# A two-block transformer step on one core: gate products in rounded parts, other banks and another order in the sparse attention, and one high part moved in the memory attention

## The chip, the cores and the metric

The kernel is one program on 1 core of a Trainium2 chip. The metric is the device time of one execution, in microseconds (us). The engines are PE (TensorE), DVE (VectorE), ACT (ScalarE), POOL (GpSimd) and SP (SyncE, which issues most of the weight loads).

## The reference, cut to what matters

`reference` runs two blocks on x of 512 tokens by 1024 features, all in float32. The first is a feed-forward layer, a mixer (retention and differential attention), memory attention and a second feed-forward layer. The second block begins with one wide product, whose parts feed sparse attention (compressed, selected and window branches), a gated recurrence ("mlstm"), a second memory attention and a merge; a feed-forward layer ends it. The change touches these lines:

```python
# memory attention of the first block: per head, a query product, its norm, softmax, values
q = rms_norm((h @ w_q).reshape(b, s, MEM_HEADS, MEM_HEAD_DIM), q_norm)
p = jax.nn.softmax(sc, axis=-1).astype(v.dtype)
# second block: gates, and the recurrence's running maximum
gb = jax.nn.sigmoid(g_nsa.reshape(B, S, NSA_GROUPS, NSA_HPG, 3))
gates = if_ml.astype(jnp.float32) + ml_gate_b[l].astype(jnp.float32)
logf = jax.nn.log_sigmoid(gates[..., ML_HEADS:])
b = jnp.cumsum(fj, axis=1).transpose(0, 2, 1)
m_t = jnp.maximum(inter, jnp.max(dlog, axis=-1))
# compressed scores of a group of four heads; with 512 tokens every block is selected
s = jnp.einsum('bsghd,bngd->bghsn', q, kc) * NSA_SCALE
y_nsa = (gb[..., 0:1] * o_cmp + gb[..., 1:2] * o_slc + gb[..., 2:3] * o_win).reshape(B, S, NSA_Q)
```

## The kernel before, in words

All activations lie transposed in SBUF. A weight panel (128 output columns, 8 tiles of 128 rows) is loaded by SP into a ring of `slot`s and split into a rounded high part and a rounded low part (`parts0` and `parts1` in turn). The high part is made by ACT (`high_part`, L2020) or by POOL (L574), the low part always by POOL (L586, or L583 and L586 in two pieces). A panel product on PE is then 24 matmuls in rounded float32: high and low against the activations' high part `hhi`, high against their low part `hlo`. Matmuls on plain float32 operands are one instruction in the code and two records in the trace.

The order on every engine is written out by hand, and semaphores count banks, panels and steps. `emptied(b, n)` lets PE wait until bank b was read n times in this stage; `Counts` and dictionaries such as `NSA` hold how often each is counted per stage.

Gates stage (`n.past(KV2)` to `n.past(GATES)`): PE makes four group products, and between them the gate product (`gate_w` against `h32`, plain float32), a cumulative sum (`lf` against `tables`, twice, and `ifp` against the identity), and columns of the result (`gate_columns`). DVE makes the running maximum in `rows`. Ahead of the stage DVE scales x by the norm (L3208).

Sparse stage: 4 groups of 4 heads. A group needs three panels (two of queries, one of keys), whose product goes to bank c % 2. ACT copies out the rounded high part (`query_or_key`), then DVE the low part (`query_low`, L3260) and frees the bank; the keys are then copied to the other 64 partitions by two DMAs of ACT's queue (`key_twins`). The selected and window branches run in 64 steps s, 16 per group. In a step PE makes `sparse_scores(s)`, DVE its minima (`sparse_minima`, L3328), ACT the exponentials (L2586), and DVE the probabilities (`sparse_probs(s - 1)`, L3340). PE turns those of step s - 2 (`turn_sparse`, L1675), ACT places them (`place_sparse`, L2013), and every fourth step has a `sparse_out` (L1690, L1693). Between them PE weaves matmuls of the next panels, whose number per step stands in `V_FILL` (group 0), `FILL` (groups 1 and 2) and a fixed 3 (group 3). The compressed branch of a group is `compressed_scores` (L1644), then DVE's front, maxima, ACT's exponential, DVE's back and division, then `turn_compressed`. The steps p = 13 to 15 of a group have no woven matmuls.

Recurrence: `spread_maxima` (L1767) brings a row of the running maximum to all partitions, once per head.

Of the kernel before, what the change touches and what calls it, by code (L numbers as in the profile page):

```python
# [27 lines left out]
P = 128  # L28
# [77 lines left out]
NSA = dict(products=16, splits=16, highs=16, free0=8, free1=10, free2=9, qkhighs=3 * GROUPS, free3=STEPS, free4=STEPS,  # L106
           free5=STEPS, free6=STEPS, free7=1 + 2 * GROUPS, twins=GROUPS, cscores=GROUPS, cmps=GROUPS, cexps=GROUPS,
           cprobs=GROUPS, cturned=GROUPS, scores=2 * STEPS, exps=2 * STEPS, probs=2 * STEPS, turned=2 * STEPS, outs=8,
           dve=7 * GROUPS + STEPS)
FILL = [(6, 0)] + [(3, 3)] * 6 + [(3, 2)] * 6  # L110
# [3 lines left out]
FREED = (0, 0, 1, 3, 3, 4, 4, 6, 5, 7, 7, 8)  # L114
CBANK, CFREED = (1, 1, 0, 1), (1, 5, 6, 9)
# [24 lines left out]
GATES = dict(outs=1, free7=1, gates=1, acts=5, free2=1, dve=4, stats=2, free3=2, turned=1, free6=1)  # L140
# [65 lines left out]
def build(nc, xT, memT, mem2T, par, con, tab, headtab, w8, w7, w4, gatew, cmpw1, cmpw2, outT):  # L206
    with ExitStack() as ctx:
# [36 lines left out]
        gate_w = sb("gate_w", KD, GATE_COLS)  # L244
# [15 lines left out]
        lf = sb("lf", 4, TT, 4)  # L260
# [26 lines left out]
        rows = hid[:, 18:22, :]  # L287
        PTr = hid[:, 8:12, :]
# [57 lines left out]
        cmp_loaded = sem("cmp_loaded")  # L346
        shifted = sem("shifted_rows_copied")
# [63 lines left out]
        zeros_set = sem("zeros_set")  # L411

# [130 lines left out]
        def _(pool):  # L543
# [107 lines left out]
            for p in range(30):  # L651
                split(p, p % RING, "act" if 10 <= p < 28 else p - 2 if p < 2 else p - 1, load=1 + p // RING, pieces=2 if p >= 8 else 1)
# [37 lines left out]
            pool.memset(ssum[:, :], 0.0).then_inc(zeros_set, 1)  # L690
            n.past(KV2)
# [35 lines left out]
        def _(pe):  # L727
# [779 lines left out]
            def gate_columns():  # L1507

                emptied(6, 1)
                emptied(3, 1)  # L1510
                for t in range(TT):
# [7 lines left out]
            pe.wait_ge(cmp_loaded, 96)  # L1519
# [17 lines left out]
            for t in range(TT):  # L1537
                mm = pe.matmul(bank[3][0:4, t * P:T], lf[:, 1, t, :], tables[:, K_CUM:K_CUM + T - t * P],
                               start=(t == 0), stop=(t == TT - 1))
            mm.then_inc(stats, 1)  # L1540
            emptied(6)
            for t in range(TT):
                pe.matmul(bank[6][0:4, t * P:T], lf[:, 2, t, :], tables[:, K_CUM:K_CUM + T - t * P],
                          start=(t == 0), stop=False)
# [63 lines left out]
            def sparse_values(q, a, b):  # L1608
# [4 lines left out]
                for m in range(a, b):  # L1613
                    t, j = (m // 4, m // 2 % 2) if m < 16 else ((m - 16) // 2, m % 2)
                    at = (0, 1, 2, 7)[t]
                    if q == 0 and m < 16 and m % 4 == 0:
                        emptied(at, (2, 2, 0, 1)[t])
# [2036 lines left out]
```

## Time and profile before

| | |
|---|---|
| median of 3 runs | 2387.17 us (2385.77 to 2392.31) |
| profiled execution, its time | 2383.35 us |
| its span | 2381.5 us |
| PE busy | 2304.9 us (97%) |
| DVE, ACT, POOL busy | 898.9, 884.1, 1029.8 us |
| gates stage (PE) | 1235.17 to 1273.16 us |
| sparse stage (PE) | 1273.16 to 1555.4 us |

The span is the profiler's stretch from first to last instruction, and the execution's own time is 1.85 us more. Times in rows are counted from the span's start. A row of the timeline has its start, its length, the engine, the line and the operation; the brackets give the idle time before it and what ended that. PEclk is the granted TensorE clock, where 1.00 is 2.4 GHz and 0.50 is 1.2 GHz.

### The profile page before, as it was taken

The page shows a single profiled execution, that of the slowest core. Times are in us where ns is not written, and L with a number is a line of the kernel's source. Part 1 is how long each engine was busy: PE and PEld are TensorE (multiplying, and loading weights), DVE is VectorE, ACT ScalarE, POOL GpSimd, SP SyncE. Part 2 cuts the span into 40 slices and gives each one's busy share as a digit, 9 for nine tenths or more (in the row PEclk, how much of TensorE's full clock was granted, in tenths as well). Part 3 has the DMA queues.
Part 4 walks back from the last instruction along what each step waited for, and adds up shares of the span by engine and source line. Part 5 has one row for each costly group of instructions (what it writes and reads, how often), then busy time and mean ns, then how long its engine had stood idle before and what let it go on. Part 6 is the DMA issues. An engine that isn't in the chain of part 4 may idle for free.

```text
span 2381.5 us, 28274 instructions
## 1 busy us (share of the span) xinstructions
PE 2304.9 (97%) x10592; PEld 1843.2 (77%) x10592; DVE 898.9 (38%) x1499; ACT 884.1 (37%) x1566; POOL 1029.8 (43%) x560
## 2 busy tenths in 40 slices
PE   7999999999999999999999999999999998999997
PEld 6888888777687788888867766677788877888886
DVE  4443424024422344533233566635511113333411
ACT  4222334245544532223323465645522234222332
POOL 3444457832362544444534422053244443444445
PEclk9999999999999999999999999999999998999998
DMA  4333334322231233323352211021123331333232
GB/s 170 96 96 96 95 94 151 118 73 66 68 98 45 73 96 97 97 88 93 102 142 83 63 38 35 18 71 62 45 89 98 96 97 54 97 97 97 83 95 96
DMA packets 81259, 206.39 MB, mean 87 GB/s; under 512 B 7440, under 2 KB 31120, under 8 KB 80912
## 3 DMA queue, kind: packets, MB, share of 16 engines
q1 hardware_dynamic: 72832, 191.92, 26.3%
q10 hardware_dynamic: 8336, 13.25, 1.9%
q8 instruction: 58, 0.95, 0.2%
q14 instruction: 33, 0.27, 0.0%
HBM read 199.71 MB, written 2.10 MB: 85 GB/s over the span
## 4 chain that ended last, share of the span: by engine, by line
PE 89%; ACT 4%; DVE 4%; POOL 1%; issue 1%; ACTq 0%; DMA 0%; DVEq 0%; POOLq 0%
PE bank L769 16%; PE bank L770 15%; PE bank L776 15%; PE bank L1071 5%; PE bank L1937 3%; PE bank L1938 3%; PE bank L1942 3%; PE bank L1304 3%; PE bank L1563 2%; PE bank L1742 2%; PE bank L1693 2%; PE bank L1664 1%; PE bank L1619 1%; PE bank L1675 1%; PE bank L1756 1%; PE bank L1848 1%
## 5 line engine op out<-in xcount | busy, mean ns | idle before, releaser
L586 POOL TENSOR_TENSOR parts<-slot,parts 128x1024 fp32r<-128x1024 f32 (+3 forms) x318 | 634.8, 1996 | 629.7 <-ACT parts L2020 628.0
L769 PE MATMUL bank<-hhi,parts 128*128 128x512 f32 x1440 | 562.3, 390 | 6.2 <-POOL parts L586 3.5
L2020 ACT ACTIVATE parts<-slot 128x1024 fp32r<-128x1024 f32 (+2 forms) x281 | 271.9, 968 | 781.7 <-PE bank L776 734.4
L770 PE MATMUL bank<-hhi,parts 128*128 128x512 f32 x1440 | 561.3, 390 | 0.0
L776 PE MATMUL bank<-hlo,parts 128*128 128x512 f32 x1440 | 356.7, 389 | 0.0
L769 PEld LDWEIGHTS bank<-hhi,parts 128*128 128x128 f32 x1440 | 270.8, 188 | 67.3 <-issue 7.0
L770 PEld LDWEIGHTS bank<-hhi,parts 128*128 128x128 f32 x1440 | 270.9, 188 | 55.7
L776 PEld LDWEIGHTS bank<-hlo,parts 128*128 128x128 f32 x1440 | 270.2, 188 | 56.1
L574 POOL TENSOR_TENSOR parts<-slot,lanes 128x1024 fp32r<-128x1024 f32 x42 | 83.5, 1988 | 285.9 <-PE bank L1563 127.0
L2866 DVE TENSOR_TENSOR silu<-silu,rinv 128x512 f32<-128x512 f32 x66 | 151.9, 2301 | 60.4 <-ACT silu L2063 60.4
L583 POOL TENSOR_TENSOR parts<-slot,parts 128x512 fp32r<-128x512 f32 x55 | 71.2, 1295 | 226.2 <-ACT parts L2020 224.6
L2864 DVE TENSOR_TENSOR ex<-bank,rinv 128x512 f32<-128x512 f32 x66 | 45.5, 689 | 234.1 <-PE bank L776 229.0
L714 POOL TENSOR_TENSOR parts<-slot,parts 128x1024 fp32r<-128x1024 f32 x24 | 59.9, 2494 | 78.6 <-ACT parts L2719 78.6
L2013 ACT ACTIVATE PT<-bank 128x128 f32<-128x128 f32 (+2 forms) x96 | 44.5, 464 | 132.8 <-PE bank L1675 98.9
L1071 PE MATMUL bank<-hhi,parts 128*128 128x512 f32 x320 | 88.9, 411 | 0.0
L2869 DVE TENSOR_TENSOR hid<-silu,bank 128x512 f32 (+1 forms) x66 | 45.4, 688 | 99.1 <-PE bank L776 98.3
L2838 DVE TENSOR_TENSOR hlo<-hid,hhi 128x512 fp32r<-128x512 f32 x42 | 41.9, 1047 | 107.9 <-ACT hhi L2112 107.9
L3470 DVE TENSOR_TENSOR ex<-silu,bank 128x512 f32<-128x512 f32 x24 | 16.5, 688 | 172.0 <-PE bank L1942 172.0
L769 PE MATMUL bank<-bigr,parts 128*128 128x512 f32 x192 | 75.4, 393 | 0.1
L770 PE MATMUL bank<-bigr,parts 128*128 128x512 f32 x192 | 74.8, 389 | 0.0
L1937 PE MATMUL bank<-hhi,parts 128*128 128x512 f32 x184 | 71.7, 389 | 1.5 <-ACT silu L2768 1.5
L1938 PE MATMUL bank<-hhi,parts 128*128 128x512 f32 x184 | 71.6, 389 | 0.0
(588 smaller groups left out, 3931.2 us busy)
## 6 DMA issues: line engine op xcount, KB each, us to landing
slot<-w SPq DMA_DIRECT2D x264, 512.0 KB, 3.5
slot<-w SPq DMA_DIRECT2D x88, 256.0 KB, 2.7
slot<-w SPq DMA_DIRECT2D x48, 448.0 KB, 3.2
hid<-w SPq DMA_DIRECT2D x8, 512.0 KB, 3.5
x<-xT ACTq DMA_DIRECT2D x4, 512.0 KB, 9.8
hid<-headtab ACTq DMA_DIRECT2D x8, 256.0 KB, 3.7
big<-cmpw ACTq DMA_DIRECT2D x4, 512.0 KB, 9.7
hid<-w SPq DMA_DIRECT2D x8, 256.0 KB, 2.6
```

The lines of the kernel that those rows point to most:

```text
L574: pool.tensor_tensor(high, w, nought.unsqueeze(2).to_broadcast([P, KD, P]), ALU.add).then_inc(highs, 1)
L586: pool.tensor_tensor(low, w, high.bitcast(F32), ALU.subtract).then_inc(splits, 1)
L769: pe.matmul(out, high[:, k, :], mhi[:, k, :], start=(start and k == 0), stop=False)
L770: pe.matmul(out, low[:, k, :], mhi[:, k, :], start=False, stop=False)
L776: mm = pe.matmul(out, high[:, k, :], mlo[:, k, :], start=False, stop=(stop and k == kt - 1))
L1071: mm = pe.matmul(out, (low if m < 16 and m % 2 else high)[:, k, :], moving, start=(m == 0), stop=(m == 23))
L1304: mm = pe.matmul(out, (low if m < 16 and m % 2 else high)[:, k, :], (mhi if m < 16 else mlo)[:, k, :], start=(m == 0), stop=(m == 23))
L1937: pe.matmul(bank[q % 2][:, :], high[:, k, :], mhi, start=(k == 0), stop=False)
L1938: pe.matmul(bank[q % 2][:, :], low[:, k, :], mhi, start=False, stop=False)
L1942: mm = pe.matmul(bank[q % 2][:, :], high[:, k, :], mlo, start=False, stop=(k == len(moving) - 1))
L2020: act.activation(parts[nth % 2][:, 0, 0:kt, :], slot[j][:, 0:kt, :], ACT.Copy).then_inc(highs, 1)
L2866: dve.tensor_tensor(silu[:, u, :], silu[:, u, :], rinv[:, :], ALU.mult).then_inc(gscaled, 1)
```

## The change

1. Gates: `gate_w` is split once by ACT and POOL, and the gate product becomes 24 rounded matmuls. The log forget gates are split by DVE into two rounded parts, the cumulative sum is made once (8 rounded matmuls) and DVE subtracts it from `ifp`. Each `spread_maxima` becomes two rounded matmuls.
2. Sparse stage, start: the third panel goes to bank 4, the first compressed scores to banks 6 and 3 (they were 7 and 1). ACT's exponential and DVE's maxima of group 0 move from ahead of the steps into steps 0 to 2.
3. Sparse stage, steps: `query_low` stands behind `sparse_probs`, `compressed_scores(g + 1)` in step 14 instead of 13 and its front in DVE's step 15, and the woven matmuls are spread otherwise (none in the steps with a `sparse_out`, 6 to 8 in most others).
4. Memory attention: `dense_high` of a head's first panel stands ahead of the load of the table and the squares.
5. Mixer: POOL waits for all probabilities before it splits panel 28.

```diff
-FILL = [(6, 0)] + [(3, 3)] * 6 + [(3, 2)] * 6
+FILL = [(6, 0), (3, 3), (0, 0)] + [(4, 3)] * 3 + [(0, 0)] + [(4, 4)] * 3 + [(0, 0), (4, 4), (4, 3)]
+LAST_FILL = [(0, 0) if p % 4 == 2 else (2, 2) for p in range(16)]
-CBANK, CFREED = (1, 1, 0, 1), (1, 5, 6, 9)
+PANEL_BANK = (0, 1, 4, 1, 0, 1, 0, 1, 0, 1, 0, 1)
+CBANKS, CFREED = ((6, 3), (7, 1), (7, 0), (7, 1)), ((0, 0), (2, 4), (4, 5), (6, 8))
@@ POOL
             for p in range(30):
+                if p == 28:
+                    pool.wait_ge(probs, n.at("probs", MIX["probs"]))
                 split(p, p % RING, "act" if 10 <= p < 28 else p - 2 if p < 2 else p - 1, load=1 + p // RING, pieces=2 if p >= 8 else 1)
...
+            pool.wait_ge(gate_highs, 1)
+            pool.tensor_tensor(gate_low[:, :, :], gate_w[:, :, :], gate_high[:, :, :].bitcast(F32), ALU.subtract).then_inc(gate_lows, 1)
@@ PE
-            pe.wait_ge(h32s, n.at("h32s"))
+            pe.wait_ge(gate_lows, 1)
             emptied(7)
-            for k in range(KD):
-                mm = pe.matmul(bank[7][0:GATE_COLS, :], gate_w[:, k, :], h32[:, k, :], start=(k == 0), stop=(k == KD - 1))
+            for m in range(24):
+                k = m // 2 if m < 16 else m - 16
+                mm = pe.matmul(bank[7][0:GATE_COLS, :], (gate_low if m < 16 and m % 2 else gate_high)[:, k, :],
+                               (hhi if m < 16 else hlo)[:, k, :], start=(m == 0), stop=(m == 23))
...
-                if p == 13 and g < GROUPS - 1:
+                if p == 14 and g < GROUPS - 1:
                     compressed_scores(g + 1)
...
-                pe.matmul(bank[2][:, :], ident[0:4, i:i + 1].to_broadcast([4, P]), rows[0:4, 1, :], start=True,
-                          stop=True).then_inc(mspreads, 1)
+                for part in range(2):
+                    mm = pe.matmul(bank[2][:, :], selectors[0:4, i:i + 1].to_broadcast([4, P]), row_parts[part],
+                                   start=(part == 0), stop=(part == 1))
+                mm.then_inc(mspreads, 1)
@@ ACT
+                if h >= 1:
+                    dense_high(2 * h + 2, 3)
                 root_table()
                 query_tile(h, 0)
-                if h >= 1:
-                    dense_high(2 * h + 2, 3)
...
+            act.activation(tables_r[:, K_CUM:K_CUM + T], tables[:, K_CUM:K_CUM + T], ACT.Copy)
+            act.activation(selectors[0:4, :], ident[0:4, 0:4], ACT.Copy)
+            act.activation(gate_high[:, :, :], gate_w[:, :, :], ACT.Copy).then_inc(gate_highs, 1)
...
             query_or_key(1)
-            compressed_exponentials(0)
             query_or_key(2)
             key_twins(2)
@@ DVE
             query_low(1)
+            query_low(2)
             compressed_front(0)
-            compressed_maxima()
-            query_low(2)
-            compressed_back(0)
-            compressed_division(0)
...
+                if s >= 1:
+                    sparse_probs(s - 1)
                 for c in panels_finished(s - 1):
                     query_low(c)
-                if s >= 1:
-                    sparse_probs(s - 1)
```

ACT at the start of the sparse stage. `rinv<-var` is the exponential of the compressed scores, `ks_r` and `silu_r` are the keys' high parts (`query_or_key(2)`), the two DMAs are `key_twins(2)`, `ex` is a step's exponential. Before:

```order
L2592 ACT_TABLE_LOAD
L2592 ACTIVATE rinv<-var 128x16x31 [waits shifted_compressed_scores]
L2541 ACTIVATE ks_r<-bank0 64x512 [waits panel_products]
L2541 ACTIVATE silu_r<-bank0 64x512
L2569 DMA ks_r<-ks_r 64x1024 [waits bank0_free]
L2570 DMA silu_r<-silu_r 64x1024
```

and in the changed kernel:

```order
L2564 ACTIVATE ks_r<-bank4 64x512 [waits panel_products]
L2564 ACTIVATE silu_r<-bank4 64x512
L2592 DMA ks_r<-ks_r 64x1024 [waits bank4_free]
L2593 DMA silu_r<-silu_r 64x1024
L2609 ACT_TABLE_LOAD
L2609 ACTIVATE ex,lanes<-sc,lanes 128x128 [waits bank4_free]
```

The keys' copies and the DMAs no longer stand behind the exponential, which now comes in step 1.

PE at steps 13 to 15 of group 0: L1675 turns, L1644 are the compressed scores, L1664 the step's scores, L1690 the first matmul of `sparse_out`. Before:

```order
L1675 MATMUL bank3<-consts,o_sb 128x128 x3
L1644 MATMUL bank7<-hid_r,silu_r 128x64 [waits bank1_free,bank7_free,bank0_free]
L1644 MATMUL bank7<-hid_r 128x64 x3
...
L1664 MATMUL bank5<-silu_r,hid_r 128x384
L1690 MATMUL bank2<-o_sb,hid 128x512 [waits bank1_free,bank2_free,bank0_free,bank7_free,bank3_free,bank6_free]
```

and in the changed kernel:

```order
L1678 MATMUL bank5<-silu_r,hid_r 128x384
L1704 MATMUL bank2<-o_sb,hid 128x512 [waits bank1_free,bank2_free,bank0_free,bank7_free,bank3_free,bank6_free]
...
L1689 MATMUL bank3<-consts,ex 128x128 [waits bank3_free]
L1658 MATMUL bank7<-hid_r,silu_r 128x64 [waits bank7_free,bank1_free,bank0_free]
L1658 MATMUL bank7<-hid_r 128x64 x3
```

The compressed scores come after step 14's scores, its `sparse_out` and its turn.

## Rows read from the trace of the kernel before

**Rows 1.** The page: span, and busy time of each engine (share, instructions).
```profile
span 2381.5 us, 28274 instructions
PE 2304.9 (97%) x10592; PEld 1843.2 (77%) x10592; DVE 898.9 (38%) x1499; ACT 884.1 (37%) x1566; POOL 1029.8 (43%) x560
```

**Rows 2.** PE's waits from 1300 to 1500 us: total, times, longest.
```profile
PE bank L1644 <- DVE hid_r L3260: 7.4, 3, 2.7
PE bank L1675 <- DVE o_sb L3340: 5.9, 4, 2.1
PE bank L1619 <- DVE silu_r L3260: 3.6, 1, 3.6
```

**Rows 3.** Stretches: length, PE busy (records), granted clock, DMA share, GB/s.
```profile
1305.30:1312.00 6.70, 6.70 (x18) 0.57 0.31 78
1373.00:1381.00 8.00, 7.73 (x41) 0.79 0.00 0
1431.00:1439.00 8.00, 8.00 (x30) 0.61 0.01 2
1491.00:1500.00 9.00, 9.00 (x38) 0.62 0.00 0
1416.00:1424.00 8.00, 7.86 (x47) 1.00 0.00 0
```

**Rows 4.** Timeline of the mixer's end, of PE, POOL and DVE.
```profile
643.61 0.55 PE L1133 MATMUL bank<-consts,o_sb 128*128 128x128 f32 x3 [2.70 <-DVE o_sb L3040]
638.56 1.89 POOL L574 TENSOR_TENSOR parts<-slot,lanes 128x1024 fp32r<-128x1024 f32 x1 [4.75 <-PE bank L1071]
638.73 1.74 DVE L3025 TENSOR_SCALAR lanes<-lanes 128x2 f32<-128x2 f32 x1
```

**Rows 5.** Timeline in the memory attention (head 1), of PE and ACT.
```profile
737.41 0.96 PE L1304 MATMUL bank<-hhi,parts 128*128 128x512 f32 x3 [1.04 <-POOL parts L586]
731.27 1.28 ACT L1991 ACT_TABLE_LOAD   x1
733.72 1.05 ACT L2020 ACTIVATE parts<-slot 128x1024 fp32r<-128x1024 f32 x1
```

**Rows 6.** Timeline of the gates stage, of PE, POOL and DVE.
```profile
1235.17 0.47 PE L769 MATMUL bank<-hhi,parts 128*128 128x512 f32 x1 [0.33 <-POOL parts L586]
1240.82 7.07 PE L1524 MATMUL bank<-hid,gate_w 128*56 128x512 f32 x16
1260.18 2.32 PE L1538 MATMUL bank<-tables,lf 128*4 128x512 f32 x8
1228.12 4.38 POOL L574 TENSOR_TENSOR parts<-slot,lanes 128x1024 fp32r<-128x1024 f32 x1 [20.10 <-DMA slot<-w]
1225.36 5.38 DVE L3208 SCALAR_TENSOR_TENSOR x<-x,params,var 128x512 f32<-128x512 f32 x8
```

**Rows 7.** Timeline of the sparse stage's start: PE, ACT, DVE, ACT's queue.
```profile
1305.27 6.57 PE L1619 MATMUL bank<-parts,hhi 128*128 128x512 f32 x16 [3.65 <-DVE silu_r L3260]
1301.86 0.62 ACT L2592 ACTIVATE rinv<-var 128x496 f32<-128x496 f32 x1 [5.42 <-DVE var L3300]
1304.42 0.69 DVE L3260 SCALAR_TENSOR_TENSOR silu_r<-bank,silu_r 64x512 fp32r<-64x512 f32 x1
1305.65 0.61 ACTq L2570 DMA_DIRECT2D silu_r<-silu_r  x1
```

**Rows 8.** DMA issues from 1300 to 1320 us: KB each, us from issue to landing.
```profile
silu_r<-silu_r ACTq DMA_DIRECT2D x1, 256.0 KB, 3.7
```

**Rows 9.** Timeline around step 14 of group 0, of PE and ACT.
```profile
1373.27 0.27 PE L1644 MATMUL bank<-hid_r,silu_r 128*128 128x64 f32 x1 [2.69 <-DVE hid_r L3260]
1372.11 0.59 ACT L2013 ACTIVATE hid<-bank 128x512 f32<-128x512 f32 x1
```

**Rows 10.** DVE's probabilities of step 39, against POOL's high part begun at 1471.49.
```profile
1473.58 2.57 DVE L3340 TENSOR_SCALAR o_sb<-o_sb,lanes,gates 128x512 f32<-128x512 f32 x1
```

**Rows 11.** Timeline of the recurrence's start, of PE.
```profile
1555.40 1.09 PE L1767 MATMUL bank<-hid,consts 4*128 4x512 f32 x2 [0.78 <-ACT hid L2013]
```

More of the change, by code:

```diff
@@ L137, in key_or_pair @@
     return (0, 1, None)[c] if c < 3 else (None, 0, 1)[c % 3]
-GATES = dict(outs=1, free7=1, gates=1, acts=5, free2=1, dve=4, stats=2, free3=2, turned=1, free6=1)
+GATES = dict(outs=1, free7=1, gates=1, acts=5, free2=1, dve=5, stats=2, free3=2, turned=1, free6=1)
 ML = dict(products=16, splits=16, highs=16, free0=6, free1=6, free4=9, free5=9, free6=1, free7=5, mspreads=4,
@@ L243, in build @@
         tables, tables_r = twofold("tables", NTAB)
-        gate_w = sb("gate_w", KD, GATE_COLS)
+        gate_w, gate_low = twofold("gate_w", KD, GATE_COLS)
+        gate_high = sbr("gate_high", KD, GATE_COLS)
+        selectors = sbr("selectors", 4)
         w2 = sb("w2", P + 64)
@@ L1537, in _ @@
             for t in range(TT):
-                mm = pe.matmul(bank[3][0:4, t * P:T], lf[:, 1, t, :], tables[:, K_CUM:K_CUM + T - t * P],
-                               start=(t == 0), stop=(t == TT - 1))
+                for part in (2, 0):
+                    mm = pe.matmul(bank[3][0:4, t * P:T], lf_r[:, part, t, :],
+                                   tables_r[:, K_CUM:K_CUM + T - t * P],
+                                   start=(t == 0 and part == 2), stop=(t == TT - 1 and part == 0))
             mm.then_inc(stats, 1)
@@ L1542, in _ @@
             for t in range(TT):
-                pe.matmul(bank[6][0:4, t * P:T], lf[:, 2, t, :], tables[:, K_CUM:K_CUM + T - t * P],
-                          start=(t == 0), stop=False)
-            for t in range(TT):
-                mm = pe.matmul(bank[6][0:4, t * P:(t + 1) * P], ifp[:, t, 0:4], ident, start=False,
-                               stop=(t == TT - 1))
+                mm = pe.matmul(bank[6][0:4, t * P:(t + 1) * P], ifp[:, t, 0:4], ident, start=True, stop=True)
             mm.then_inc(turned, 1)
@@ L1559, in sparse_panel @@
                     pe.wait_ge(splits, n.at("splits", ahead.get("splits", 0) + p + 1))
-                    emptied(c % 2, ahead.get(f"free{c % 2}", 0) + earlier(c))
+                    emptied(at, ahead.get(f"free{at}", 0) + earlier(c))
                 for m in range(a, b):
@@ L1635, in compressed_scores @@
                 for c in (3 * g, 3 * g + 1) if g == 0 else (3 * g + 1, 3 * g + 2):
-                    emptied(c % 2, earlier(c) + 1)
-                emptied(CBANK[g], CFREED[g])
-                emptied(7, 1 + 2 * g if g else 0)
-                if g == 0:
-                    emptied(3)
+                    emptied(PANEL_BANK[c], earlier(c) + 1)
+                for b, count in zip(CBANKS[g], CFREED[g]):
+                    emptied(b, count)
                 for t in range(TT):
@@ L1643, in compressed_scores @@
                         at = (t % 2 * 4 + a) * 64
-                        mm = pe.matmul(bank[7 if t < 2 else CBANK[g]][:, at:at + 64], q_heads[g % 2][a][:, t * P:(t + 1) * P],
+                        mm = pe.matmul(bank[CBANKS[g][t // 2]][:, at:at + 64], q_heads[g % 2][a][:, t * P:(t + 1) * P],
                                        kc_both[:, g, :], start=True, stop=True)
@@ L2565, in key_twins @@
             def key_twins(c):
-                b, (first, second) = c % 2, k_parts[c // 3 % 2]
+                b, (first, second) = PANEL_BANK[c], k_parts[c // 3 % 2]
                 act.wait_ge(free[b], n.at(f"free{b}", earlier(c) + 1))
@@ L2609, in _ @@
                         key_twins(c)
+                if p == 1 and g < GROUPS:
+                    compressed_exponentials(g)
                 if 2 <= s < STEPS + 2:
@@ L3235, in _ @@
             dve.wait_ge(dves, n.at("dve", 4))
-            dve.wait_ge(stats, n.at("stats", 1))
-            dve.tensor_tensor(rows[0:4, 2, :], bank[3][0:4, :], rows[0:4, 1, :], ALU.add).then_inc(free[3], 1)
+            dve.tensor_tensor(rows[0:4, 2, :], rows[0:4, 2, :], rows[0:4, 1, :], ALU.add).then_inc(dves, 1)
             dve.wait_ge(stats, n.at("stats", 2))
@@ L3292, in compressed_front @@
                     dve.tensor_tensor(c, s_parts[:, :, :, 1, :], c, ALU.add).then_inc(free[b], 1)
-                dve.wait_ge(free[7], n.at("free7", 2 * g + 2 if g else 1))
-                dve.wait_ge(free[CBANK[g]], n.at(f"free{CBANK[g]}", CFREED[g] + 1))
+                for b, count in zip(CBANKS[g], CFREED[g]):
+                    dve.wait_ge(free[b], n.at(f"free{b}", count + 1))
             def compressed_maxima():
```

82 lines of the change are left out of this document (50 added, 32 removed).

## The prediction, as recorded before the run

> **What bounds the kernel now.** The page comes first: PE is busy for 2304.9 of 2381.5 us [rows 1]. So a gain is either PE work taken away, PE idle time closed, or PE's clock kept up; nothing that only another engine does can bring more. Next comes the list of PE's waits. Of some 77 us of idle time in the whole span, 16.9 us lie between 1300 and 1500 us, in the sparse stage, and all of it is DVE's: 3.6 us at the first value panel (L1619), 7.4 us in three waits of the compressed scores (L1644) for `query_low`, 5.9 us in four waits of the turns (L1675) for the probabilities [rows 2]. Third, the granted clock of the stretches behind these waits. After the 3.65 us stall it is 0.57 in the mean over 6.7 us, and after the three compressed waits 0.79, 0.61 and 0.62 over 8, 8 and 9 us, where it is 1.00 after a 1.07 us wait [rows 3]. These are stretches partly at 1.2 GHz. PE has work in nearly all of them, so a share below one is work that runs at half speed: 6.7 x 0.43 = 2.9 us, 8 x 0.21 = 1.7, 8 x 0.39 = 3.1 and 9 x 0.38 = 3.4, together 11.1 us. The four stalls (3.6 + 7.4 = 11.0 us) so cost about twice their length. Outside the stage I read the timeline at single waits: 2.70 us at the end of the mixer [rows 4], three of 1.0 us in the memory attention, of which the first is shown [rows 5], and the plain float32 products in the gates stage and the recurrence [rows 6, 11].
>
> **Mixer's end.** PE waits 2.70 us for a turn's probabilities. POOL's split of panel 28 begins at 638.56, and DVE's operation on 128x2 elements, begun at 638.73, takes 1.74 us [rows 4]; it lasts until POOL's high part is through at 640.45. The two exclude each other. The change lets POOL wait for all 16 probabilities. DVE's chain is then about 3 us shorter, and PE gets to the turn at 640.9. The split moves from 638.56 to about 643 and takes 4.5 us; PE needs panel 28 only after the last attention products, some 9 us later, so the move is free. Were the split late, the wait would come back there. Gain 2.6 us (0 to 2.7).
>
> *A rule beside it.* The Trainium skill, "SBUF — State Buffer", on the port pair that DVE and GpSimd share, says that it is an exclusive lock, held for the whole instruction by whoever starts first. Rows 4 agree: 1.74 us against 0.17 us for the same operation elsewhere. By that rule the whole wait goes, 2.7 us instead of 2.6, and the sum would be 27.5 instead of 27.4 us; the same rule makes the loss in the gates stage below the full 1.3 us. Neither changes a chance.
>
> **Memory attention.** ACT has the table load at 731.27 and makes the high part of the head's first panel only at 733.72. It now makes it first, 2.45 us earlier. POOL's low part follows it and is what PE waits for, 1.04 us at 737.41 [rows 5]; 2.45 exceeds 1.04, so the wait goes. The squares behind it come about 1 us later than now in ACT's order, but the second half of them waits for PE's own panel anyway, and the first half has 1.6 us of ACT's idle time ahead of it. Three heads: 3.1 us (2 to 3.1).
>
> **Gates stage.** One rounded matmul of 512 columns costs (1240.82 - 1235.17) / 24 = 0.235 us. The gate product takes 7.0 us as 16 records and becomes 24 matmuls, 5.65 us: -1.35. The cumulative sum goes from two times 2.15 us (2.32 us less the overlap with what follows [rows 6]) to eight matmuls of 512 to 128 columns, 2560 in all, 1.2 us: -3.1. DVE's chain behind it gets one more pass of 4x512, 0.7 us, and had 1.1 us of slack before `gate_columns`: nothing. The new load is POOL's. Its low part of `gate_w` (448 columns, about 1.1 us by the split's 512-column pieces) must wait for ACT's three copies, so it starts at about 1225.7, in DVE's run of 5.38 us from 1225.36. POOL's high part that began at 1228.12 took 4.38 us instead of 1.9, and ended 1.76 us after that run [rows 6]. So the new operation is done only at about 1231.8 and the first panel's split 1.1 us later than now, and PE already waits 0.33 us for it: +1.15 (0 to 1.3). Stage: -3.3.
>
> **Sparse stage, start.** PE was ready for the values at 1301.62 and began at 1305.27, because bank 0 had to be freed by `query_low(2)`, which stood behind ACT's exponential at 1301.86 [rows 7]. With bank 4 in its place PE goes on at once. Then it meets another wait: the step's scores need the key copies. ACT copies the keys from 1301.8 to 1303.0, DVE's two low parts take 1.38 us, the second DMA is issued 0.5 us after the first, at 1304.9, and lands 3.7 us later [rows 7, 8], at 1308.6. PE has 20 matmuls (4.7 us) to do until then and is there at 1306.3: 2.3 us of waiting. Now the scores start at 1312.6, then at 1308.6, a gain of 4.0 us if the clock stays up. A wait of 2.3 us is hardly shorter than the three of 7.4 / 3 = 2.5 us that were followed by half speed, which would cost up to 3 us; so I take half of that off, 2.5 us. The bounds are 1 (clock down) and 6.5 (3.6 + 2.9, no new wait).
>
> **Sparse stage, group boundaries.** Stall and half speed of the three compressed waits are 7.4 + 8.2 = 15.6 us. One step later `query_low` has ended long before. What takes the place: in step 14 `sparse_out` needs the turned step 11, which ACT places until 1372.70 [rows 9], while PE, not held up at 1370.6, is there at 1371.3: 1.4 us. Then DVE has front (1.5 us), maxima (1.4 us) and three steps' minima and probabilities in three steps with little PE work; I count another 0.9 us. That is 2.3 us of the 5.2 per boundary: gain 15.6 - 6.9 = 8.7 us (3 to 15.6).
>
> **Sparse stage, turns.** Four waits, 5.9 us. Two had `query_low` ahead of the probabilities (1.4 us of DVE), two a POOL split that stretched them, as one of 0.5 us to 2.57 us [rows 10]. The order ends the first kind. The woven work puts 7 or 8 matmuls (1.6 to 1.9 us) into steps that had 5 or 6, so that panels end where short probabilities follow: gain 5.0 (2 to 5.9). Steps with `sparse_out` lose 1.4 us of cover; ACT's placing had about 1.1 us of slack there, so about nothing.
>
> **Recurrence.** Each of four `spread_maxima` takes 1.02 us to the next start [rows 11] and becomes two rounded matmuls, 0.47 us: -2.2. The extra DVE splits (1.4 us) lie at the start, under the wait for the key copies.
>
> **Sum.** 2.6 + 3.1 + 3.3 + 2.5 + 8.7 + 5.0 + 2.2 = 27.4 us. The profiled execution took 2383.35 us (span 2381.5), so it becomes 2356.0. The median of the runs is 3.8 us above it, 2387.17: forecast 2360 us.
>
> **The rivals.**
> *The stalls move on (0.20).* At the boundaries DVE and ACT chains set the pace whatever the order, and the key copies hold the start. For it: 16.9 us of waits all name DVE. Against: the orders that put `query_low` ahead of what PE waits for are what the change turns round. The sparse stage then gives 5 instead of 16.2: 2383.35 - 16.2 = 2367.1, or 2371 by the median.
> *All goes (0.14).* No residual waits and full clock: 6.5 + 15.6 + 5.9 in the stage and 11.2 outside, 39.2 us: 2344, or 2348.
> *The stage gives nothing and the rest little (0.04):* 0 to 7 us, 2381 to 2387.
> *Slower (0.04).* Ten steps with `sparse_out` in the groups 1 to 3 lose all their woven matmuls. What is left in them is `sparse_out` on 64 columns of weights, turns, and waits for ACT's placing. If PE's clock fell to 1.2 GHz there, a fall would cost 2.8 us, the mean of 2.9, 1.7, 3.1 and 3.4 from rows 3, and the boundaries would keep their stalls: of the 27.4 us, 18.7 would be left. From 7 falls on (19.6 us) it decides; with all ten it is 28 - 18.7 = 9.3 us slower, 2392.7, or 2396 by the median. Against it: behind the 1.07 us wait at 1416 us, with a `sparse_out` in the stretch, the clock is 1.00 [rows 3].
>
> The Trainium skill, "TensorE: Matmul & The Clock Gate", section "A second HAM failure mode: psum-queue depth-cycling", says that frequent short idle times between groups of matmuls that cycle through PSUM banks can make the clock swing between its two levels. That speaks for this rival, since the change adds such spots; rows 3 show the swing only behind the long stalls.
>
> **How the numbers follow.** The main case has 0.58, with its own range 2353 to 2367 from the bounds above taken half way. The range 2349 to 2373 holds it, the moved stalls and half of the largest case. The three runs before spread over 6.5 us, so 0.3% (7 us) is about what a measurement can tell from no change. Faster by more than that: 0.58 + 0.20 + 0.14 = 0.92; within 0.3%: 0.04; slower: 0.04.
>
> **What would show it.** In the profile after: the wait of the turn at 643.6 and the 1.0 us waits of the memory attention gone; the first split of the gates stage ending about 1.1 us later against the end of the value product, and a longer wait of PE there; PE's first scores waiting for a DMA of ACT's queue; a wait of `sparse_out` in steps 14 of 1 to 1.5 us; granted clock near 1.00 from 1360 us on. The prediction is wrong if the clock is at half speed in places without a stall now, or if the first panels' split or the key copies cost more than 3 us.

## The result and the profile after

The changed kernel takes 2354.98 us (median, 2353.19 to 2355.68) where the kernel before took 2389.28 us beside it (2385.77 to 2392.31): a ratio of 0.9852, with a 95% interval of 0.9835 to 0.9869. The forecast was 2360 us. The profiled execution took 2355.28 us (span 2353.5); from here on I compare its trace with that of before, which took 2383.35 us (span 2381.5).

The two traces are 28.0 us of span apart, the medians 34.3 us. The trace of before is that of a fast execution: the lowest of the 41 timed runs of that kernel is 2384.46 us, and the mean granted clock of the 37 of them beside the experiments is 0.979 to 0.986, where the trace has 0.987. So what follows explains 28.0 us. Where a usual run of the kernel before spends the other 6 us no trace shows; the lower clock points to half speed.

The page, its first rows (span, busy time of each engine):

```profile
span 2353.5 us, 28283 instructions
PE 2292.9 (97%) x10592; PEld 1843.1 (78%) x10592; DVE 917.7 (39%) x1503; ACT 886.5 (38%) x1569; POOL 1030.8 (44%) x561
```

PE's busy time fell by 12.0 us, its idle time by 16.0. PE's waits from 1273 to 1473 us, which answer to [rows 2], the three largest (total, times, longest):

```profile
PE bank L1704 <- ACT PT L2031: 3.3, 3, 1.5
PE bank L1678 <- DMA silu_r<-silu_r: 2.4, 1, 2.4
PE bank L1667 <- ACT big L2031: 1.5, 1, 1.5
```

The three causes of [rows 2] are gone: no row of `compressed_scores` (now L1658), and DVE's probabilities hold up no turn (L1689). What is left waits for ACT's placing, once for the key copies, and twice, 0.6 us together, for DVE's minima (not shown). The stretches that answer to [rows 3] (length, PE busy (records), PEld, DVE, ACT, POOL, granted clock, DMA share, GB/s), the first behind the wait for the key copies, the next three behind waits of `sparse_out`:

```profile
1303.50:1310.20 6.70, 6.70 (x33) 5.73 (x34) 3.81 (x13) 2.59 (x9) 4.81 (x3) 1.00 0.30 81
1363.70:1371.70 8.00, 7.89 (x50) 5.29 (x51) 5.55 (x17) 3.77 (x15) 0.32 (x1) 1.00 0.00 0
1416.00:1424.00 8.00, 7.89 (x50) 5.28 (x51) 5.67 (x17) 3.76 (x15) 1.68 (x2) 1.00 0.01 2
1468.50:1477.50 9.00, 8.86 (x57) 5.88 (x57) 7.71 (x20) 4.58 (x17) 1.48 (x1) 1.00 0.03 10
```

Four times 1.00, where before it was 0.57 to 0.79 behind the long waits. The whole stretch of the sparse steps, from the first turn of the compressed scores (L1667) to the first `spread_maxima` (L1784), ran from 1337.47 to 1555.40 us before. After:

```profile
1328.41 0.63 PE L1667 MATMUL bank<-consts,ssum 128*128 128x128 f32 x4 [1.54 <-ACT big L2031]
1528.41 0.69 PE L1784 MATMUL bank<-hid_r,selectors 4*128 4x512 f32 x2 [0.89 <-ACT hid L2031]
```

217.9 us became 200.0. The matmuls in it are the same (1133 records in both), so the difference of PE's busy time in it measures the clock: 198.8 us before, 189.9 after. Idle time fell from 19.1 to 10.1 us. So of 17.9 us, 9.0 were waits and 8.9 half speed.

That is the stretch alone. A window with granted clock c over L us loses L x (1 - c). Added up over windows of 5 us, the whole trace loses 25.6 us before and 22.8 after:

```
us of half speed          before   after
0 to 650 us                  0       1.7
650 to 1200 us               0       3.4
1200 to 1300 us              3.4     5.1
1300 to 1560 us             11.9     0
behind 1560 us              10.2    12.6
```

What the sparse stage gained, other places lost for the most part. That the edits did this is not shown: the run with step 14 alone (below) has the code of before in its first 1300 us, and its trace loses 1.7, 3.4 and 3.4 us in the first three rows.

Where the 28.0 us of span came from, by the starts of the same instructions in both traces, beside the forecast's terms:

```
stretch                                     forecast   in the two traces
program start to the mixer's end               0            -0.6
mixer's end (the turn, L1147)                  2.6           2.7
memory attention to the second values          3.1          -0.3
gates stage                                    3.3           3.6
sparse stage, start                            2.5           3.6
sparse steps (boundaries 8.7, turns 5.0)      13.7          17.9
recurrence                                     2.2           1.6
behind it                                      0            -0.5
sum                                           27.4          28.0
```

The sum was right partly because errors cancel, which is luck: the sparse steps and the sparse start together gave 5.3 us more than forecast, and the memory attention 3.4 us less.

At the mixer's end, POOL's split now begins behind the probabilities, and the turn at 641.50 us waits for nothing:

```profile
643.39 1.89 POOL L584 TENSOR_TENSOR parts<-slot,lanes 128x1024 fp32r<-128x1024 f32 x1 [8.85 <-DVE o_sb L3062]
```

In the gates stage, the timeline of POOL, DVE and PE, which answers to [rows 6]:

```profile
1223.65 1.64 POOL L704 TENSOR_TENSOR gate_w_r<-gate_w,gate_high 128x448 fp32r<-128x448 f32 x1 [17.86 <-ACT gate_high L2507]
1226.24 2.01 POOL L584 TENSOR_TENSOR parts<-slot,lanes 128x1024 fp32r<-128x1024 f32 x1 [0.95 <-DMA slot<-w]
1256.04 1.31 PE L1556 MATMUL bank<-tables_r,lf_r 128*4 128x512 f32 x8
1259.85 2.09 DVE L3260 TENSOR_TENSOR_SCAN hid<-hid 4x512 f32<-4x512 f32 x1
1262.80 1.91 PE L1528 MATMUL bank<-consts,hid 4*128 4x4 f32 x16 [0.63 <-DVE hid L3263]
```

POOL's new operation was done at 1225.3, not at 1231.8. The split behind it took 2.01 us where it took 4.38, and PE's 0.33 us wait for the first split is gone instead of 1.1 us longer. DVE's scan took 2.09 us where it took 1.21; two low parts of POOL, from 1258.32 to 1260.86 us, now reach into it, where POOL was idle before; no run has one without the other. PE waited 0.63 us for DVE's chain, and in the 5 us from 1265 the clock is lower:

```profile
1265.00:1270.00 5.00, 5.00 (x16) 3.97 (x15) 1.67 (x4) 2.23 (x3) 1.89 (x1) 0.66 0.13 32
```

And the wait at the start of the sparse steps, forecast as 2.3 us:

```profile
1303.50 0.66 PE L1678 MATMUL bank<-ks_r,qs_r 128*128 128x128 f32 x4 [2.43 <-DMA silu_r<-silu_r]
```

### The profile page after: what moved, and what is told of

Read it like the earlier page. It is cut to its first block and busy times, and to the rows that moved or that the text cites. A ratio compares the mean times of both kernels' runs of the same rounds, so it can differ in the third digit from the quotient of the medians.

```text
span 2353.5 us, 28283 instructions
## 1 busy us (share of the span) xinstructions
PE 2292.9 (97%) x10592; PEld 1843.1 (78%) x10592; DVE 917.7 (39%) x1503; ACT 886.5 (38%) x1569; POOL 1030.8 (44%) x561
```

## The experiments

Twelve kernels, each timed beside the kernel before on the same chip. "Slower than the changed kernel" is the difference of two medians, and the changed kernel's runs are those at the top of this text, which have their own runs of the kernel before. The theories: **A**, the order (step 14, `query_low` behind the probabilities) took the stalls away, and with them the half clock; **B**, the new spread of the woven matmuls did it; **C**, the clock goes its own way.

**The steps' three edits, undone one by one.**

```diff
-                if p == 14 and g < GROUPS - 1:
+                if p == 13 and g < GROUPS - 1:
                     compressed_scores(g + 1)
@@ DVE
-                if s < STEPS - 16 and s % 16 == 15:
+                if s < STEPS - 16 and s % 16 == 14:
                     compressed_front(s // 16 + 1)
```

> The changed kernel with the compressed scores of the next group back in step 13 and their front in DVE's step 14; all else as changed. Theory A (the boundaries' stall and the half clock behind it made up what the sparse steps gave): each of three compressed scores waits 2.4 us or more for query_low again, since query_low now stands behind the probabilities, and the clock is at half behind it; about 5 us a boundary come back, less the 1 to 1.5 us wait of sparse_out: 2366 to 2372 us. Theory B (the new spread of the woven matmuls gave it, the step hardly matters): 2355 to 2359 us, with granted clock 1.00. Theory C (stall back, but the clock stays up, since the clock follows the load of the whole step and not a stall): 2359 to 2363 us.

2376.45 us, ratio to before 0.9949 (0.9933 to 0.9966): 21 us slower than the changed kernel, beyond every theory; the trace, of its fastest run, has 17.2 us of that in the steps. PE's waits in its steps, and two stretches behind them:

```profile
PE bank L1658 <- DVE hid_r L3286: 12.6, 3, 4.8
1365.00:1375.00 10.00, 9.82 (x38) 6.53 (x38) 3.37 (x12) 0.00 (x0) 0.00 (x0) 0.55 0.00 0
1423.00:1433.00 10.00, 9.68 (x36) 6.46 (x38) 3.51 (x12) 0.00 (x0) 0.00 (x0) 0.55 0.01 2
```

The wait is 4.2 us in the mean, not 2.5. In this kernel `query_low` stands behind the probabilities and up to 8 woven matmuls stand in a step; with both as before (all three edits undone, below) it is 2.4 us. Which of the two lengthens it no run shows. The granted clock is 0.55 over 10 us behind the first two waits, longer than behind any in [rows 3].

```diff
+                for c in panels_finished(s - 1):
+                    query_low(c)
                 if s >= 1:
                     sparse_probs(s - 1)
-                for c in panels_finished(s - 1):
-                    query_low(c)
```

> The changed kernel with query_low ahead of sparse_probs in DVE's order again; all else as changed. Theory A: two to four turns per group wait up to 1.4 us for the probabilities again, 2 to 4 us in all, no half clock: 2357 to 2359 us. Theory B (the spread of the woven matmuls covers it): 2355 us, within 1 us.

2355.55 us, 0.9860 (0.9839 to 0.9882): no difference, and the same waits of the turns as in the changed kernel, two of 0.6 and 1.3 us at the end of the steps. With the new spread the order gives nothing (theory B for this part).

```diff
-FILL = [(6, 0), (3, 3), (0, 0)] + [(4, 3)] * 3 + [(0, 0)] + [(4, 4)] * 3 + [(0, 0), (4, 4), (4, 3)]
-LAST_FILL = [(0, 0) if p % 4 == 2 else (2, 2) for p in range(16)]
+FILL = [(6, 0)] + [(3, 3)] * 6 + [(3, 2)] * 6
+LAST_FILL = [(2, 1) for p in range(16)]
```

> The changed kernel with the numbers of woven matmuls per step as before (6 or 5 in each step, 3 in the last group). Theory A (order gave nearly all): 2356 to 2359 us, a few waits of turns of 0.5 to 1 us, and the wait of sparse_out in step 14 unchanged. Theory B (the spread gave it): 2363 us or more, with waits of the turns and half clock in the steps of groups 1 to 3.

2366.41 us, 0.9901 (0.9881 to 0.9922): 11.4 us slower, as theory B has it. The longest wait of a turn is back, with a clock of 0.79 in the 8 us behind it; the clock is also down at the end of the steps, where no single wait is longer than 1.3 us (three of the kernels below, which keep the new spread, show a shorter fall at that place too, of 1.7 to 3.4 us of half speed):

```profile
1458.93 0.66 PE L1689 MATMUL bank<-consts,ex 128*128 128x128 f32 x4 [2.13 <-DVE o_sb L3366]
1459.00:1467.00 8.00, 8.00 (x40) 5.64 (x41) 4.47 (x16) 3.02 (x11) 0.00 (x0) 0.79 0.00 1
1530.00:1545.00 15.00, 12.43 (x39) 7.63 (x40) 6.44 (x14) 6.48 (x12) 8.43 (x4) 0.55 0.08 26
```

All three edits undone together:

> All three of these edits undone together in the changed kernel: step 13, query_low first, the old spread. Every theory that places the 17.9 us between the first turn of the compressed scores and the recurrence in these three edits expects them back: 2372 to 2374 us, with granted clock about 0.6 to 0.8 behind the three compressed waits. If it is under 2368 us, part of the 17.9 us comes from what the stage now starts with (a clock that is up, or an earlier start).

2366.19 us, 0.9909 (0.9881 to 0.9938): 11.2 us slower than the changed kernel, less than with the first edit undone alone, and below the 2368 us under which, as the expectation says, part of the 17.9 us comes from elsewhere. In the traces below the three edits together are worth 14.9 us of the stretch (214.87 against 200.00); the other 3.1 us come with the rest of the change, or with the clock of one execution. And in the kernel before, step 14 alone:

```diff
-                if p == 13 and g < GROUPS - 1:
+                if p == 14 and g < GROUPS - 1:
                     compressed_scores(g + 1)
@@ DVE: compressed_front at s % 16 == 15 (14), compressed_maxima at s % 16 == 0 (15)
```

> The kernel before with one edit alone: the compressed scores of the next group in step 14, their front in DVE's step 15 and the maxima in step 16, with the old order of query_low and the old spread of woven matmuls. The forecast's term (8.7 us for the boundaries): 2378.5 us where the kernel before has 2387.4. Theory D, from the run with all three edits undone and the one with the old spread (214.9 and 210.0 us for the sparse steps, 4.9 us between them): about 5 us, 2382 us, since a turn still waits 2.1 us for the probabilities and the clock falls behind it. Theory B (the step by itself gives nothing): 2386 us or more.

2379.39 us, 0.9955 (0.9940 to 0.9970): 10.8 us faster than before by the ratio, nearer to the forecast's 8.7 than to theory D's 5. Its trace shows 5.6 us between the two marks, as theory D has it, with half clock at their end. The ten runs spread over 14.7 us, so the two prices are not told apart. This is the stretch between the marks, one row of the windows for each kernel (before, step 14 alone, all three undone, old spread, step 13, `query_low` first, changed):

```profile
1337.47:1555.40 217.93, 198.78 (x1133) 144.32 (x1133) 143.51 (x463) 127.57 (x393) 46.27 (x29) 0.96 0.12 35
1340.26:1552.61 212.35, 196.04 (x1133) 142.26 (x1133) 145.09 (x463) 128.27 (x393) 48.87 (x30) 0.98 0.13 36
1327.76:1542.63 214.87, 196.34 (x1132) 143.41 (x1133) 144.69 (x463) 127.70 (x393) 46.23 (x29) 0.97 0.12 35
1328.52:1538.49 209.97, 195.99 (x1133) 141.00 (x1133) 151.54 (x463) 128.15 (x393) 49.06 (x30) 0.98 0.12 36
1327.94:1545.18 217.24, 199.55 (x1132) 148.10 (x1133) 153.18 (x463) 128.12 (x393) 45.80 (x29) 0.94 0.12 35
1329.55:1529.31 199.76, 189.69 (x1132) 140.43 (x1133) 143.88 (x463) 128.44 (x393) 45.84 (x29) 1.00 0.13 38
1328.41:1528.41 200.00, 189.88 (x1132) 140.38 (x1133) 152.82 (x463) 128.58 (x393) 45.86 (x29) 1.00 0.13 38
```

Length, then PE's busy time. Length less busy time is waiting: 19.2, 16.3, 18.5, 14.0, 17.7, 10.1, 10.1 us. Busy time over 189.7 is half speed: 9.1, 6.3, 6.6, 6.3, 9.9, 0, 0.2 us. Of these, only the two with step 14 and the new spread keep the clock up throughout. Neither edit's worth is its own: step 14 is worth 17.2 us with the new spread (217.24 against 200.00) and 5.6 with the old one (217.93 against 212.35); the new spread is worth 10.0 us with step 14. With step 13 the new spread and the new order of `query_low` together cost 2.4 (217.24 against 214.87), which no run takes apart. The trace of the old spread is that of its slowest run; the lowest times of the two kernels, 2362.96 and 2353.19 us, are 9.8 us apart.

**Mixer and memory attention.**

```diff
-                if p == 28:
-                    pool.wait_ge(probs, n.at("probs", MIX["probs"]))
```

> The changed kernel without POOL's wait for all probabilities ahead of the split of panel 28. Theory A (the shared use of the port by DVE and POOL made the 2.70 us wait): the wait of the turn at 643 us is back, POOL's split begins near 639 us and stretches DVE's operation on 128x2 elements again: 2357 to 2358 us. Rival (the wait had another cause, as the order of loads): 2355 us and no wait. The changed kernel has 1.66 us of PE idle time at 420 us and half clock at 715 and 740 us that the one before does not have; if they come with this edit they go here.

2358.31 us, 0.9865 (0.9841 to 0.9889). The wait is back, 2.68 us; POOL's split begins at 640.05 us, ahead of the probabilities. The stretch from 599.8 to 703.4 us (103.6) is 2.9 us longer. Theory A. The half clock in the memory attention does not come from this edit: it stands at 760 to 770 us here (0.78 and 0.87). The idle time at 420 us is no effect of the change either: the trace of before has it too, 1.7 us.

```diff
-                if h >= 1:
-                    dense_high(2 * h + 2, 3)
                 root_table()
                 query_tile(h, 0)
+                if h >= 1:
+                    dense_high(2 * h + 2, 3)
```

> The changed kernel with dense_high of a head's first panel behind the table load and the squares again. Theory A: three waits of 1.0 us are back, and the granted clock of the memory attention is 1.00 throughout as before, so that only 1.5 to 2.5 of the 3.1 us come back: 2356.5 to 2357.5 us. Rival (the half clock at 715 and 740 us has nothing to do with this edit): 2358 us, and it stays.

2360.57 us, 0.9881 (0.9857 to 0.9904), above both theories. The rows of the waits, from 704 to 783 us:

```profile
PE bank L1318 <- POOL parts L596: 2.1, 2, 1.0
PE bank L1381 <- POOL parts L596: 1.0, 1, 1.0
```

Three waits of 1.0 us are back, and the one of 0.95 us that the changed kernel has at 794 us (a turn, L1352, for DVE's probabilities) is gone: PE comes there about 3 us earlier with the edit. From 702.4 us to the first sparse scores the trace is 2.4 us longer; the medians differ by 5.6 us, and what the other 3 us are no trace shows (its trace is that of its fastest run, 2356.80 us). Half clock appears twice in this stretch with the edit undone too, so the rival holds: it is not this edit's.

**Gates stage.**

```diff
-            pool.wait_ge(gate_highs, 1)
-            pool.tensor_tensor(gate_low[:, :, :], gate_w[:, :, :], gate_high[:, :, :].bitcast(F32), ALU.subtract).then_inc(gate_lows, 1)
@@ PE
-            pe.wait_ge(gate_lows, 1)
+            pe.wait_ge(gate_highs, 1)
```

> The changed kernel without POOL's low part of gate_w (left out: the low part of the gate weights; the high part is used in its place, so as many matmuls). Theory A (POOL wins the port, DVE's scaling of x is what is stretched, and nobody waits for that): DVE's eight operations take 5.4 us instead of 13.8, POOL's first split ends 1.6 us earlier, PE gains nothing: 2355 us. Rival (the forecast's term, PE waits for POOL): 0.5 to 1.2 us faster.

2355.51 us, 0.9857 (0.9831 to 0.9883): no change. The kernel leaves out the low part of the gate weights and makes as many matmuls. DVE's run, POOL's first split and PE's wait of this kernel, and DVE's run of the changed one:

```profile
1221.03 5.39 DVE L3228 SCALAR_TENSOR_TENSOR x<-x,params,var 128x512 f32<-128x512 f32 x8
1223.71 4.46 POOL L584 TENSOR_TENSOR parts<-slot,lanes 128x1024 fp32r<-128x1024 f32 x1 [20.23 <-DMA slot<-w]
1230.84 0.47 PE L781 MATMUL bank<-hhi,parts 128*128 128x512 f32 x1 [0.34 <-POOL parts L596]
```

```profile
L3230 DVE SCALAR_TENSOR_TENSOR x<-x,params,var x8: 737/1997/2884, 1223.6 to 1236.6; 128x512 f32<-128x512 f32 x8
```

Without the new operation POOL comes into DVE's run, is held up to its end (1226.42; its operation takes 4.46 us) and PE waits 0.34 us. With it, the minimum, median and maximum of DVE's operations are 737, 1997 and 2884 ns: DVE is held up, operation by operation, 13.8 us for eight, POOL hardly (2.01 and 2.34 us for high parts that take 1.9 elsewhere in the stage, 2.67 and 2.73 for low parts that take 2.4), and nobody waits for DVE there. The forecast's loss of 1.15 us had its sign from the wrong winner. The Trainium skill, "SBUF — State Buffer", section "Who interferes with whom", states that whoever starts first has the shared port pair for the whole instruction and the other fully blocks. The two traces agree on the blocking, and show that one side can win many turns in a row, DVE's run in one and POOL's in the other. Why POOL wins here is open: DVE's first operation began at 1223.55 us, 0.10 us ahead of POOL's.

```diff
-            h_panel(3, bank[1][:, :], between=gate_columns)
+            h_panel(3, bank[1][:, :])
+            gate_columns()
```

> The changed kernel with gate_columns behind the whole of the fourth gates panel instead of between its parts (1.8 us later). Theory A (the 0.63 us wait for DVE's chain and the short matmuls behind it made the clock fall to half until 1269 us): the wait goes and the clock stays at 1.00, 2 to 3 us faster: 2352 to 2353 us. Theory B (the fall has nothing to do with the wait: it comes with the 16 tiny matmuls): 0.6 us faster, the half clock follows gate_columns to its new place.

2356.46 us, 0.9857 (0.9833 to 0.9880): no gain. Its windows, and those of the changed kernel for the same stretches:

```profile
1255.00:1270.00 15.00, 15.00 (x80) 11.70 (x79) 6.05 (x9) 7.55 (x8) 8.88 (x6) 1.00 0.46 122
1300.00:1310.00 10.00, 8.40 (x34) 6.91 (x35) 4.15 (x16) 2.60 (x9) 4.69 (x3) 0.83 0.21 72
```

```profile
1255.00:1270.00 15.00, 14.37 (x70) 11.01 (x69) 6.05 (x10) 7.31 (x8) 6.33 (x4) 0.89 0.35 96
1300.00:1310.00 10.00, 7.57 (x38) 6.10 (x36) 5.65 (x16) 3.88 (x10) 5.83 (x4) 1.00 0.41 107
```

Wait and half clock at `gate_columns` are gone, as theory A said; but the clock now falls behind the wait for the key copies, 2.44 us here and 2.43 there. Two other traces show that the wait at `gate_columns` does not make the fall. The kernel without POOL's wait for the probabilities has the wait of 0.63 us and no half clock behind it, and its clock is 0.66 behind the wait for the key copies, again 2.43 us:

```profile
1263.45 1.92 PE L1526 MATMUL bank<-consts,hid 4*128 4x4 f32 x16 [0.63 <-DVE hid L3261]
1255.00:1270.00 15.00, 14.37 (x78) 11.17 (x77) 6.48 (x12) 8.20 (x9) 6.81 (x5) 1.00 0.38 106
1300.00:1310.00 10.00, 7.57 (x23) 6.07 (x23) 3.11 (x8) 2.29 (x6) 4.53 (x4) 0.66 0.29 93
```

And the kernel with all three mends (below) has `gate_columns` moved and no wait there, and half clock all the same:

```profile
1255.00:1270.00 15.00, 15.00 (x74) 11.59 (x73) 6.05 (x9) 7.04 (x7) 8.87 (x6) 0.89 0.47 129
```

So this run's theory A (the wait makes the fall) is refuted, and its theory B (the fall comes with `gate_columns`) as well, since the run with `gate_columns` moved has full clock there. What is left is theory C. In the ten traces that have the 2.4 us wait for the key copies, the clock falls in one place of the two and never in both: at 1260 to 1270 us in eight, behind the key copies in two. What links the two no run shows.

**Mends.** More woven work ahead of the first scores:

```diff
-V_FILL = [(8, 8)] * 4 + [(12, 0), (0, 0)] + [(6, 5)] * 6 + [(6, 0)]
+V_FILL = [(8, 4), (8, 4), (8, 8), (8, 6)] + [(12, 0), (0, 0)] + [(6, 5)] * 6 + [(6, 0)]
...
-            woven(0, 20, sparse_values)
+            woven(0, 30, sparse_values)
```

> The changed kernel with 30 instead of 20 woven matmuls of the values ahead of the first step's scores, and four fewer in steps 0 and 1 and two fewer in step 3. The wait for the DMA of the key copies (2.43 us) is filled with 2.35 us of work. Theory A (that wait is idle time that work can fill, and steps 0 to 3 have cover enough): 2.2 us faster, 2353 us. Rival (the steps 0 to 3 lose their cover and wait for DVE's probabilities, or the second value panel waits for POOL's split, which ends at 1301.2 us): 0 to 1 us faster, with new waits of the turns before 1325 us or of the values at 1302 us.

2354.05 us, 0.9854 (0.9837 to 0.9870), not to be told from the changed kernel. In its trace the wait is gone, and from `gate_columns` to the turn of the compressed scores it is 63.4 instead of 65.6 us: 2.3 us, theory A.

```diff
-LAST_FILL = [(0, 0) if p % 4 == 2 else (2, 2) for p in range(16)]
+LAST_FILL = [(0, 0) if p % 4 == 2 else (2, 1) for p in range(16)] + [(2, 2)] * 3
```

> The changed kernel with 12 of the 48 woven matmuls of the last group taken from its steps (3 instead of 4 each) and put into the three steps behind the last scores, where PE has waits of 0.58, 1.25, 0.83 and 0.89 us. Theory A (those waits are hidden, and steps with 3 woven matmuls keep their cover): 2 to 2.8 us faster, 2352 to 2353 us. Rival (the last group's turns wait for the probabilities instead, as with the old spread, where a turn waited 2.13 us and half clock stood behind it): 0 to 3 us slower.

2356.08 us, 0.9864 (0.9845 to 0.9882). The four waits at the end shrink from 3.6 to 0.9 us, but the stretch between the marks only from 200.0 to 199.2. A wait for DVE in the last group grows from 0.52 to 0.74 us, and PE's busy time in the stretch is 1.1 us more (191.0), for which I have no explanation. Neither theory's size.

> The changed kernel with all three mends: 30 woven matmuls of the values ahead of the first scores, gate_columns behind the whole of the fourth gates panel, and 12 woven matmuls in the three steps behind the last scores. Theory A (idle time filled is time gained): 2.3 (measured in the profile of the first), 0.6 for the wait at gate_columns, and 2 for the end of the steps, 4.9 us: 2350 us. Theory C (the clock's falls move to other places and take it back, as behind the moved gate_columns): 2353 to 2355 us, with a stretch at half clock between 1260 and 1310 us or behind 1525 us that the changed kernel does not have.

2351.94 us, 0.9829 (0.9815 to 0.9842), against 0.9852 for the changed kernel: 3.0 us less by the medians and 5.5 by the ratios, the fastest of all, but the intervals overlap. So theory A's 4.9 us are neither shown nor excluded for the total. Its profiled execution, the slowest of five with 2355.58 us (the other four took 2350.11 to 2351.99), has all three idle places filled or nearly so. In this execution the clock took it back elsewhere. The row of 85 us behind 1905 us in it and, in the second fence, in the changed kernel:

```profile
1905.00:1990.00 85.00, 76.70 (x328) 64.64 (x328) 23.13 (x37) 35.15 (x57) 32.37 (x17) 0.82 0.20 60
```

```profile
1905.00:1990.00 85.00, 75.68 (x338) 62.89 (x336) 24.70 (x39) 37.05 (x59) 35.39 (x18) 0.86 0.22 69
```

These rows stand for that execution only: 3.4 us of half speed more than in the changed kernel. Theory A holds for the waits; what theory C takes from the total in a usual run is open.

## Why the prediction was right, and where it was off

**What bounds the kernel** held: nothing gained that was not PE's waiting, PE's work or PE's clock, and the step stretch splits into waits and half speed as the forecast had split it.

**The number.** 2360 us was forecast and 2355 measured. The sum of 27.4 us fits the 28.0 us between the traces. The step from the profiled execution to the median, 3.8 us, was taken from the kernel before, whose trace is faster than all its timed runs; the changed kernel's median lies 0.3 us below its trace. These 4 us are most of the 5 by which the forecast came out high.

**Mixer's end:** 2.6 forecast, 2.7 in the traces, and the experiment puts it back. Right in mechanism and size.

**Memory attention:** 3.1 forecast, the three waits went, but the traces show -0.3. A new wait of 0.95 us for DVE's probabilities took part of it; the forecast had followed ACT's squares and not DVE's chain at the stage's end. And the clock fell twice, where the trace of before shows no fall:

```profile
715.00:720.00 5.00, 5.00 (x20) 4.01 (x19) 1.63 (x4) 1.49 (x2) 2.52 (x2) 0.66 0.26 75
740.00:745.00 5.00, 5.00 (x19) 4.28 (x18) 1.28 (x2) 1.27 (x1) 0.47 (x1) 0.70 0.35 105
```

That is 1.7 and 1.5 us of half speed, with no wait in either. With the edit undone the clock falls as well. It falls too in the trace of the run with step 14 alone, whose memory attention is that of before:

```profile
760.00:770.00 10.00, 8.97 (x36) 7.56 (x36) 1.62 (x4) 4.58 (x7) 3.62 (x3) 0.66 0.33 105
```

So most of what is missing depends on which executions were traced; from the experiment the edit is worth 2.4 us.

**Gates stage:** 3.3 forecast, 3.6 measured, by other terms: the gate product took 5.5 us (1238.35 to 1243.88, -1.5), the cumulative sum 1.3 instead of 4.3. The loss of 1.15 us for POOL did not come, and PE's old wait of 0.33 went. In its place stand DVE's scan, stretched to 2.09 us, the wait of 0.63 and about 1.7 us of half speed, which comes and goes without the wait. The step of this term that failed was "had 1.1 us of slack before `gate_columns`: nothing": 1.1 less the added pass of 0.7 left 0.4 us, and the scan beside POOL's low parts took 0.9 us more, so 0.5 us were missing and PE waited 0.63.

**Sparse start:** 2.5 forecast, 3.6 measured. The wait was there, 2.43 us for 2.3. I had halved the gain for a clock that might fall; it stayed up, which is the 4.0 us case. It fell behind the same wait in two of ten traces, by 1.7 and 3.4 us, so half of 3 us was more than the mean of what these show.

**Boundaries and turns:** 13.7 forecast, 17.9 measured. The waits at the boundaries came to 5.7 us instead of 6.9, no turn waits where 0.9 was left, other waits in the last group and at the end shrank by about 1 us, and half speed gave 8.9 instead of 8.2. But the two terms, 8.7 and 5.0, are no separate things. The forecast priced the turns in waits only; with step 14 in and the old spread back, the traces lose 3.9 us to waits and 6.1 to the clock. This term was mis-sized most, 5.0 for 10.0. And the order of `query_low`, to which it gave part of its gain, is worth nothing once the new spread is in.

**Recurrence:** 2.2 forecast, 1.6 measured: mechanism right, 0.40 us gained each time instead of 0.55.

**The rivals.** The stalls did not move on: `sparse_out` took 3.3 us of waits for 13.3. The slower case needed falls in steps with `sparse_out` and no woven matmuls: in all nine kernels with the new spread and step 14 no 5 us from 1310 to 1520 us have a clock under 0.97. The fall comes, in three of the nine, only at the end of the steps.

**Open:** why the clock falls in one execution and not in another. Up to 1200 us ten of the profiled kernels have the same code. In the memory attention each shows one or two falls, of 1.5 to 1.8 us, between 710 and 725, 735 and 745 or 760 and 770 us, in different combinations; the trace of before has none. No run here controls that, and it is as large as what the last mends can give.

## What to carry to other kernels

Price a long stall on PE (here over 2 us, among short matmuls) at its length and at up to as much again for the clock behind it; then read PE's busy time over the same instructions in both kernels, which shows the clock's share by itself. Do the same for the whole trace before crediting it: here the stage gained 11.9 us of half speed and the trace 2.8. And ask whether the trace is a usual run: compare its time and clock with those of the timed runs. Edits that protect the same engine from stalls are not additive: undo each from the full version and add each to the old one before giving any of them a price. An idle stretch that is filled may give nothing in the total while the clock's falls move, so a mend of 1 to 2 us has to be judged on its stretch of the trace and not on the medians.

## What was not expected of the hardware

The same wait for the key copies, 2.4 us, was followed by a granted clock of 1.00 in eight traces and of 0.83 and 0.66 in the 10 us around and behind it in two, and these two are the ones without half clock at 1260 to 1270 us. Behind all nine waits of `compressed_scores`, of 2.3 to 4.8 us in three kernels, the clock was 0.55 to 0.79 over 8 to 10 us. In a contest of POOL and DVE, one added POOL operation of 1.64 us in front went with another winner for the following 12 us: eight DVE operations took 13.8 instead of 5.4 us, and POOL's 1024-column operation 2.0 instead of 4.4.
